# Gate and up products of six FFNs with weight tiles stationary, tokens moving in turns from two halves

## The reference, cut to what matters

```python
def _rmsnorm(x, g):
    x32 = x.astype(jnp.float32)
    y = x32 * lax.rsqrt(jnp.mean(x32 * x32, axis=-1, keepdims=True) + NORM_EPS)
    return (y * g.astype(jnp.float32)).astype(x.dtype)

def _swiglu(h, w_gate_up, w_down):
    gu = jnp.einsum('bsd,df->bsf', h, w_gate_up)
    g, u = gu[..., :FF], gu[..., FF:]
    return jnp.einsum('bsf,fd->bsd', jax.nn.silu(g) * u, w_down)
```

## Time and profile before

| | us |
|---|---|
| median of 3 runs | 1983.0 (1982.34 to 1984.53) |
| the profiled execution, its own time | 1981.93 |
| its span in the profile | 1979.7 |
| PE busy, share of the span | 1947.5 (98%) |
| PE weight loads busy | 1684.7 (85%) |
| DVE, ACT busy | 1233.1 (62%), 1109.0 (56%) |

### The profile page before, as it was taken

The page is one execution under the profiler, slowest core; times in us unless marked ns, Lnnn a source line. Parts: engine busy times, 40 slices in busy tenths (PEclk is TensorE's granted clock), DMA queues, the critical chain, the costliest instruction groups (busy, mean ns, idle before and its releaser), DMA issues.

```text
span 1979.7 us, 25169 instructions
## 1 busy us (share of the span) xinstructions
PE 1947.5 (98%) x9627; PEld 1684.7 (85%) x9627; DVE 1233.1 (62%) x1721; ACT 1109.0 (56%) x1682; POOL 36.3 (2%) x60
## 2 busy tenths in 40 slices
PE   8999999999999999999999999999999999999999
PEld 7888888888888888888887888888888888888888
DVE  6576665565767655655567765655555566756653
ACT  6576555455765644645467665554454466665552
POOL 0000100000000000000000000000000000000000
PEclk9999999999999999999999999999999999999999
DMA  7555666555556665566664345665666664545663
GB/s 261 163 158 171 188 198 194 196 183 174 155 177 204 200 199 197 186 202 192 197 174 144 123 160 158 188 196 196 197 192 197 197 192 138 181 143 167 195 198 138
DMA packets 258214, 359.76 MB, mean 182 GB/s; under 512 B 16908, under 2 KB 152288, under 8 KB 258096
## 3 DMA queue, kind: packets, MB, share of 16 engines
q1 hardware_dynamic: 256016, 352.75, 56.1%
q0 software_dynamic: 2080, 5.41, 0.9%
HBM read 357.04 MB, written 1.06 MB: 181 GB/s over the span
## 4 chain that ended last, share of the span: by engine, by line
PE 90%; DVE 5%; ACT 3%; issue 1%; POOL 1%; DMA 0%; SPq 0%; DVEq 0%; ACTq 0%
PE M L801 27%; PE M L803 27%; PE M L802 27%; PE AUX L843 3%; DVE WL L1303 2%; ACT WH L1082 1%; PE AUX L857 1%; PE AUX L1055 1%; PE AUX L1033 1%; PE AUX L979 1%; DVE SM L1452 1%; ACT TMP L1115 0%; DVE TMP L1409 0%; PE AUX L994 0%; PE AUX L985 0%
## 5 line engine op out<-in xcount | busy, mean ns | idle before, releaser
L1303 DVE TENSOR_TENSOR WL<-RAW,WH 128x1024 fp32r<-128x1024 f32 x669 | 815.7, 1222 | 583.1 <-ACT WH L1082 580.1
L1082 ACT ACTIVATE WH<-RAW 128x1024 fp32r<-128x1024 f32 x669 | 704.8, 1055 | 591.5 <-PE M L803 583.0
L801 PE MATMUL M<-WH,Bh 128*128 128x512 f32 x1792 | 698.7, 390 | 2.3 <-DVE WL L1303 2.3
L802 PE MATMUL M<-WL,Bh 128*128 128x512 f32 x1792 | 680.0, 379 | 0.0
L803 PE MATMUL M<-WH,Bl 128*128 128x512 f32 x1792 | 679.9, 379 | 0.0
L801 PEld LDWEIGHTS M<-WH,Bh 128*128 128x128 f32 x1792 | 339.4, 189 | 49.2 <-DVE WL L1303 2.8
L803 PEld LDWEIGHTS M<-WH,Bl 128*128 128x128 f32 x1792 | 339.2, 189 | 48.2
L802 PEld LDWEIGHTS M<-WL,Bh 128*128 128x128 f32 x1792 | 339.8, 190 | 42.6
L1111 ACT ACTIVATE AS<-M,KEEP 128x256 f32<-128x256 f32 x132 | 55.4, 471 | 93.1 <-PE M L803 89.4
L801 PE MATMUL M<-WH,MTh 128*128 128x512 f32 x128 | 53.0, 414 | 0.0
L802 PE MATMUL M<-WL,MTh 128*128 128x512 f32 x128 | 48.5, 379 | 0.0
(11 more groups left out here) (415 smaller groups left out, 2496.5 us busy)
## 6 DMA issues: line engine op xcount, KB each, us to landing
RAW<-in_ffn_w_in SPq DMA_DIRECT2D x352, 256.0 KB, 3.3
RAW<-in_w_in SPq DMA_DIRECT2D x104, 512.0 KB, 3.6
RAW<-in_w_gate_up SPq DMA_DIRECT2D x176, 256.0 KB, 3.3
RAW<-in_ffn_w_out SPq DMA_DIRECT2D x88, 512.0 KB, 3.8
RAW<-in_w_down SPq DMA_DIRECT2D x44, 512.0 KB, 3.8
RAW<-in_x_w_kv SPq DMA_DIRECT2D x32, 512.0 KB, 3.6
RAW<-in_even_w_in SPq DMA_DIRECT2D x24, 512.0 KB, 3.8
RAW<-in_odd_w_in SPq DMA_DIRECT2D x24, 512.0 KB, 4.0
```

What stands on the lines that cost most here:

```text
L801: e.matmul(out, s.hi, wh, start=s.at0, stop=False)
L802: e.matmul(out, s.hi, wl, start=False, stop=False)
L1082: e.activation(p.WH[:, h, 0:s.size], p.RAW[:, i, 0:s.size], ACT.Copy).then_inc(k.w_hi, 1)
L1303: e.tensor_tensor(p.WL[:, h, 0:s.size], p.RAW[:, s.u % NRAW, 0:s.size], hi.bitcast(F32), ALU.subtract).then_inc(k.w_lo, 1)
```

## The change

The gate and up products of all six FFNs change roles. The stationary operand is a 128x128 tile of weights, the moving one is all 256 tokens of B for one kt. One kt is then 4 weight tiles (`s.t` is gate or up, `j` one of two tiles of 128 columns) by 3 matmuls of 256 columns, 12 in all. The result has hidden columns on partitions, as the down product needs it, and the transposes of the hidden values are gone. The tokens move by turns from the two halves of 128 (`woven`), except in the FFN named f2a0 (the second FFN of layer 0 of the second block), where they move in plain sequence.

As tokens now lie on the free axis, r can't be a scalar of a partition. A step `rb` makes a tile RB with r of all tokens on every partition: two float32 matmuls with r as a broadcast stationary operand against the identity, in PE's list at 3.5 kt after the norm, and a copy on ACT. DVE multiplies the gate part with RB, ACT takes Silu in place, DVE multiplies by the up part (without r), ACT writes the high part and DVE the low part. The r of the up part is applied in the residual step, per token, together with the scale. The memory tokens and the last norm's gain are loaded into TMP buffers instead of tiles of their own.

```diff
+    def chunk_w(self, name, region, nk, lab):
+
+
+        self.bank_use[2 * self.pair] += 1
+        self.bank_use[2 * self.pair + 1] += 1
+        c = Chunk(name, self.pair, [self.bank_use[2 * self.pair], self.bank_use[2 * self.pair + 1]])
+        self.pair ^= 1
+        kt = 0
+        while kt < nk:
+            u = self.unit(name)
+            kn, ncol, _ = self.units[u]
+            for kk in range(kn):
+                for half in range(2):
+                    s = self.add("mw", self.now + 0.5 * half, 3)
+                    s.c, s.kt, s.u, s.kk, s.t, s.ncol = c, kt, u, kk, half, ncol
+                    s.at0, s.final = kt == 0, kt == nk - 1
+                    s.unit_end = half == 1 and kk == kn - 1
+                    s.src = self.made[lab, kt]
+                    s.hi, s.lo = (x[:, kt, :] for x in region)
+                    c.mms.append(s)
+                kt += 1
+                self.now += 1
+            c.done = u + 1
+        c.end = self.now
+        return c
+
...
             s = self.add("ff", c.end, 0)
-            s.c, s.norm, s.i = c, self.norms[lab_in], c_
-            s.silu = [self.AS[:, (c_ % 2) * 2 + t, 0:256] for t in range(T)]
-            s.h = [HB[:, (c_ % 3) * 2 + t, :] for t in range(T)]
-            blocks = [s.h[t][:, q * P:(q + 1) * P] for q in range(2) for t in range(T)]
-            self.turn(c.end + 2.0, "bank", s, blocks, A, 2 * c_, None, lab_mid, 2 * c_)
-        self.residual(down, A, KF, lab_mid, scale, gain, lab_next, final=final)
+            f = self.add("fh", c.end + 1.2)
+            o = self.add("fl", c.end + 2.6)
+            s.c, s.rb, s.past, s.g = c, rb, past[c_ % 2], HB[:, c_ % 2, :]
+            f.c, f.s, f.past, f.h = c, s, past[c_ % 2], HB[:, 2 + c_ % 2, :]
+            o.f = f
+            f.hi, o.lo = (x[:, 2 * c_:2 * c_ + 2, :].rearrange("p k c -> p (k c)") for x in A)
+            past[c_ % 2] = o
+            for q in range(2):
+                self.made[lab_mid, 2 * c_ + q] = o
+        self.residual(down, A, KF, lab_mid, rb, gain, lab_next, final=final)
...
+        elif s.kind == "mw":
+            c = s.c
+            h = s.u % NHL
+            if s.kk == 0 and s.t == 0:
+                e.wait_ge(k.w_lo, s.u + 1)
+            if s.src not in seen:
+                seen.add(s.src)
+                e.wait_ge(k.aux_out[s.src.bank], s.src.use)
+            if s.at0 and c.use[s.t] > 1:
+                e.wait_ge(k.m_out[c.banks[s.t]], c.use[s.t] - 1)
+            for j in range(2):
+                out = p.M[c.banks[s.t]][:, 256 * j:256 * j + 256]
+                row = slice(s.kk * s.ncol, (s.kk + 1) * s.ncol)
+                name = p.unit_names[s.u]
+                wh, wl = (x[:, h, row][:, 256 * s.t + P * j:256 * s.t + P * j + P] for x in (p.WH, p.WL))
+                xh, xl = (x if name == "f2a0" else woven(x) for x in (s.hi, s.lo))
+                e.matmul(out, wh, xh, start=s.at0 and j == 0, stop=False)
+                e.matmul(out, wh, xl, start=False, stop=False)
+                i = e.matmul(out, wl, xh, start=False, stop=s.final and j == 1)
+            if s.unit_end:
+                i.then_inc(k.w_used, 1)
+        elif s.kind == "rb":
+            e.wait_ge(k.r_made, s.norm.n)
+            if s.use > 1:
+                e.wait_ge(k.aux_out[b], s.use - 1)
+            for t in range(T):
+                i = e.matmul(aux[:, t * P:(t + 1) * P], s.norm.r[:, t:t + 1].to_broadcast([P, P]), ident, start=True, stop=True)
+            i.then_inc(k.aux_full[b], 1)
...
-                e.activation(s.silu[t], banks[t][:, 0, :], ACT.Silu, scale=r[t]).then_inc(k.silu_made, 1)
+            e.wait_ge(k.m_out[s.c.banks[0]], s.c.use[0])
+            e.activation(s.g, s.g, ACT.Silu).then_inc(k.silu_made, 1)
+        elif s.kind == "fh":
+            e.wait_ge(k.m_out[s.c.banks[1]], s.c.use[1])
+            e.activation(s.hi, s.h, ACT.Copy).then_inc(k.ff_hi, 1)
+        elif s.kind == "rb":
+            e.wait_ge(k.aux_full[b], s.use)
+            e.activation(p.RB, aux[:, 0:T * P], ACT.Copy).then_inc(k.aux_out[b], 1)
...
         elif s.kind == "res":
+            if s.rb is not None:
+                e.wait_ge(k.rs_made, s.rb.n)
             for t in range(T):
                 x = halves(p.X[:, t, s.half * 512:(s.half + 1) * 512])
-                e.scalar_tensor_tensor(out=x, in0=banks[t], scalar=s.scale, in1=x, op0=ALU.mult,
+                f = 1.0 if s.rb is None else s.rb.rs[:, t:t + 1]
+                e.scalar_tensor_tensor(out=x, in0=banks[t], scalar=f, in1=x, op0=ALU.mult,
...
         elif s.kind == "ff":
-            for t in range(T):
-                e.wait_ge(k.silu_made, 2 * (s.n - 1) + t + 1)
-                e.scalar_tensor_tensor(out=s.h[t], in0=banks[t][:, 1, :], scalar=r[t], in1=s.silu[t], op0=ALU.mult,
-                                       op1=ALU.mult).then_inc(k.m_out[c.banks[t]], 1)
+            if s.past is not None:
+                q = s.past.f.c
+                e.wait_ge(k.m_out[q.banks[1]], q.use[1])
+            e.wait_ge(k.aux_out[s.rb.bank], s.rb.use)
+            rb = p.RB.rearrange("p (h i) -> p h i", h=2).unsqueeze(1).to_broadcast([P, 2, 2, P])
+            tiles, apart_tiles = (tiles_n, apart_n) if s.n in p.natural else (tiles_w, apart_w)
+            rb = rb if s.n not in p.natural else p.RB.unsqueeze(1).to_broadcast([P, 2, 256])
+            e.tensor_tensor(tiles(s.g), apart_tiles(p.M[c.banks[0]]), rb, ALU.mult).then_inc(k.m_out[c.banks[0]], 1)
+        elif s.kind == "fh":
+            if s.past is not None:
+                e.wait_ge(k.ff_lo, s.past.n)
+            e.wait_ge(k.silu_made, s.s.n)
+            tiles, apart_tiles = (tiles_n, apart_n) if s.n in p.natural else (tiles_w, apart_w)
+            e.tensor_tensor(tiles(s.h), apart_tiles(p.M[c.banks[1]]), tiles(s.s.g), ALU.mult).then_inc(k.m_out[c.banks[1]], 1)
+        elif s.kind == "fl":
+            e.wait_ge(k.ff_hi, s.f.n)
+            e.tensor_tensor(s.lo, s.f.h, s.f.hi.bitcast(F32), ALU.subtract).then_inc(k.ff_lo, 1)
+        elif s.kind == "rb":
+            e.tensor_scalar(s.rs, s.norm.r, s.scale, None, ALU.mult).then_inc(k.rs_made, 1)
...
-                    e.dma_start(s.MX[:, t, n * 512:(n + 1) * 512],
+                    e.dma_start(p.TMP[2 * t + n],
...
-                e.dma_start(p.NF[:, n * 512:(n + 1) * 512],
+                e.dma_start(p.TMP[4 + n],
```

More of the change, by code:

```diff
@@ L176, in halves, with apart_w, apart_n, tiles_n @@
     return x.rearrange("p (h i) -> p h i", h=2)
+def apart_w(bank):
+    return bank[:, :].rearrange("p (j i h) -> p j h i", j=2, h=2)
+def apart_n(bank):
+    return bank[:, :].rearrange("p (j c) -> p j c", j=2)
+def tiles_n(x):
+    return x.rearrange("p (j c) -> p j c", j=2)
+def tiles_w(x):
+    return x.rearrange("p (j h i) -> p j h i", j=2, h=2)
 BANKED = ("turn", "tq", "ret_s", "ret_o", "st_z", "st_s", "st_o", "cu1", "cu2", "df_s", "pt", "df_o", "hg_s", "hg_o",
-          "cx_s", "cx_pt", "cx_o", "gains")
+          "cx_s", "cx_pt", "cx_o", "gains", "rb")
 HALVED = ("turn", "st_o", "hg_o", "cx_o")
 LATER = {
-    "conv": (0.0, 0.9), "turn": (0.5, 1.0), "tq": (0.5, 0.0), "gains": (0.5, 1.0), "rope": (0.0, 0.6), "ff": (0.0, 0.5),
+    "conv": (0.0, 0.9), "turn": (0.5, 1.0), "tq": (0.5, 0.0), "gains": (0.5, 1.0), "rope": (0.0, 0.6), "ff": (0.7, 0.0), "fh": (0.7, 0.0), "rb": (0.4, 0.0),
     "hq": (0.0, 1.3), "ret_s": (0.0, 0.7), "ret_o": (0.9, 1.5), "rg": (0.0, 0.6), "st_z": (0.7, 1.9), "st_p": (0.0, 0.5),
@@ L349, in turn_x, with residual @@
             self.norm(at + (2.5 if gain is not None else 0.5), lab, sq, ss)
-    def residual(self, name, region, nk, lab, scale, gain, lab_next, final=False):
+    def residual(self, name, region, nk, lab, rb, gain, lab_next, final=False):
         ss = self.small(4)
@@ L362, in residual @@
             s = self.add("res", c.end, 0)
-            s.c, s.half, s.scale = c, n, scale
+            s.c, s.half, s.rb = c, n, rb
             if final:
@@ L369, in ffn @@
     def ffn(self, gate, down, lab_in, lab_mid, scale, gain, lab_next, A, HB, final=False):
+        nm = self.norms[lab_in]
+        rb = self.add("rb", nm.at + 3.5)
+        rb.norm, rb.scale, rb.rs = nm, scale, self.small(T)
+        past = [None, None]
         for c_ in range(FF // 256):
-            c = self.chunk(gate, self.B, 0, KD, lab_in)
+            c = self.chunk_w(gate, self.B, KD, lab_in)
             s = self.add("ff", c.end, 0)
-            s.c, s.norm, s.i = c, self.norms[lab_in], c_
-            s.silu = [self.AS[:, (c_ % 2) * 2 + t, 0:256] for t in range(T)]
-            s.h = [HB[:, (c_ % 3) * 2 + t, :] for t in range(T)]
-            blocks = [s.h[t][:, q * P:(q + 1) * P] for q in range(2) for t in range(T)]
-            self.turn(c.end + 2.0, "bank", s, blocks, A, 2 * c_, None, lab_mid, 2 * c_)
-        self.residual(down, A, KF, lab_mid, scale, gain, lab_next, final=final)
+            f = self.add("fh", c.end + 1.2)
[8 more added lines that the diff above has]
```

(41 more changed lines are left out.)

1 line of the change is left out of this document (removed).

## The result

The changed kernel takes 1991.0 us (median of 6, 1989.8 to 1991.8) against 1982.7 for the kernel before in the same comparison (6 runs). The ratio is 1.0039, 95% interval 1.0026 to 1.0052: slower by 0.4%, or 8 us. The profiled execution has a span of 1989.5 against 1979.7.

What follows compares the result with a forecast made beforehand. PE was taken to bound the kernel through the time from one matmul to the next. The terms -28.8 - 2.1 + 2.7 + 3.6 + 21.1 + 9.2 gave +5.7 us, a median of 1988.7, range 1972 to 2014.

Steps and rivals of the forecast that it cites:

- the likeliest case: The whole kernel at the summed forecast, with or without a half clock: 1988.7 us, own range 1983 to 1995, chance 0.60.
- Turns: Gate and up parts: 66 turns of four transposes each, 0.436 a turn, are removed from PE: -28.8 us.
- Waits at turns: First turns of two FFNs: PE no longer waits for DVE's values, 1.41 and 0.70: -2.1 us.
- rb's matmuls: Each FFN's rb step: two float32 matmuls, run as two each, add 0.45 per FFN: +2.7 us.
- The wait at rb: First FFN: PE stands at rb until POOL, issuing small DMAs first, has written r: +3.6 us.
- Rival 4: First FFN: PE's clock falls in rb's wait, adding 2 to 3 us: 1991; no separate chance, inside the 0.60 case.
- Woven pace: Five woven FFNs: 256-column matmuls take 0.112 each, two replacing one of 0.216: +21.1 us.
- The second rival: Gate and up matmuls: load stays hidden, PE bound by the stream at 0.109: 1974, 0.5% faster; chance 0.20.
- Plain pace: f2a0, in plain sequence: 256-column matmuls take 0.1167 each, as the narrow matmuls do: +9.2 us.
- since these move the same tile: f2a0: ground for giving its matmuls the narrow matmuls' 0.1167, as both move B in plain sequence.
- The first rival: All six FFNs: weaving doesn't help at 128 columns, so all run at 0.1167: +24.6 more, 2013; chance 0.14.
- DVE and ACT at nothing: Gate and up chunks: DVE's 27 us of extra work is covered by 583 us idle before its splits, costing nothing.

Runs made afterwards that it cites:

- e7: e3 plus four transposes of the identity per gate and up chunk where the turns were, results unused; 2008.7 us, ratio 1.0132 to the kernel before.
- e3: Changed kernel with f2a0 woven too and POOL making r of the first FFN before its small loads; 1977.2 us, ratio 0.9970 to the kernel before.
- e2: Changed kernel with POOL making r of the first FFN before issuing its small loads; 1987.2 us, ratio 1.0018 to the kernel before.
- e1: Changed kernel with f2a0's tokens woven like the other FFNs; 1983.5 us, ratio 1.0001 to the kernel before.
- e4: Changed kernel with gate and up matmuls moving 240 columns instead of 256, loads and counts the same; 1983.7 us in one run.
- e5: Changed kernel with all six FFNs moving tokens in plain sequence; 2033.6 us, ratio 1.0256 to the kernel before.
- e6: Changed kernel with five FFNs moving even tokens, then odd ones, f2a0 still plain; 2594.4 us in one run.
- e8: e3 with tokens by turns from places 64, 32, 16, 8, 4 or 2 columns apart, one distance per FFN; 1985.8 us in one run.

## Why the prediction was right, point by point

The forecast was +5.7 us on the kernel before, and the runs show +8.3, inside the likeliest case's own range (1983 to 1995) and on the side forecast. The mechanism was right: the weight load takes back most of what the transposes gave. That the number came so near is in part luck, since two costs were put too low (3.5 and 1.7) and two others erred the other way (1.6 and 0.7).

- **Turns, -28.8:** held. e7 puts them back for 28.8 in the FFNs.
- **Waits at turns, -2.1:** held, as far as it can be read alone. gu0 without its new wait (e3) gained 1.48, where 1.41 was counted. f1a0 gained 1.39, of which 0.70 was counted; the other 0.7 is the wait at line 857, which the sum did not have.
- **rb's matmuls, +2.7:** held. In e2 the four matmuls at 243.84 are 0.11 apart.
- **The wait at rb, +3.6:** held, 3.49, with POOL as releaser. It came from counting places in PE's and POOL's lists, not from any row that showed a wait.
- **Rival 4, the half clock, 2 to 3 us:** happened, and cost 1.7. It was given inside the likeliest case but not put into the sum. The two levels that the prediction names in GHz stand in the traces as granted clocks of 1.00 and 0.50. At 1.00 matmuls of 512 columns start 0.216 apart, 2.4 columns a ns, and at 0.50 0.427 apart, 1.2 columns a ns (e1, from 1692.19 to 1693.90: 1.71 for four).
- **Woven pace, 0.112:** held, 0.1117, so +19.5 in place of +21.1. The 0.112 is the distance that loads keep in the float32 rows, 0.111 to 0.112, and e4 and the distances between loads in the changed kernel's trace bear out that it paces these matmuls too. The second rival is out. Its 0.109 (0.2184 for two) was an estimate, and in no run did an FFN go at that pace. Woven matmuls with a load of 0.19 took 0.1117 (e3: 111 or 112 ns), the transposes with their loads of 0.14 took 0.109, and half of the 0.216 of 512 columns is 0.108. The 2.7 ns from 0.109 to 0.1117 are worth 5280 x 0.0027 = 14 us here, more than the whole result.
- **Plain pace, 0.1167:** the term that was mis-sized. f2a0 ran at 0.120, so it cost 528 x (0.240 - 0.216) = 12.7 in place of 9.2. The step that failed is "since these move the same tile": the narrow matmuls move it with a load of 8 columns beside them, these with one of 128. e4 shows that the plain pace follows the number of moving columns (16 fewer took off 0.0080), so it is the reading that slowed, by 3% against the narrow matmuls. Whether the large load beside it is why was not tested.
- **The first rival** (weaving over 128 columns doesn't help) is out by e1 and e5.
- **DVE and ACT at nothing:** held, the new matmuls waited 0.0 for WL. DVE's extra work was 36 and not 27 us, and the idle time before its splits covered it.

With the measured terms the sum is -28.8 - 2.1 + 2.7 + 3.5 + 1.7 + 19.5 + 12.7 = +9.2, and +8.5 with the wait at line 857. The FFNs of the trace show +8.8 and the medians +8.3.

## What to carry to other kernels

Making weights stationary and moving only 256 columns gave up the cover over the weight load: here a matmul of 256 columns costs 0.1117 where half of one of 512 costs 0.108, and that ate 19.5 of the 28.8 us of the transposes in five FFNs (it would be 23.4 in six). A new step in an in-order list waits for the latest of its inputs, so look up when each input is made before placing it (r came 3.5 us late because POOL issued small loads first); moving those loads and weaving the sixth FFN turned a loss of 0.4% into a gain of 0.3%. The order in which fp32r columns are read is a price of its own, here 0.1117 to 0.233 a matmul, and it must be measured for the order used.

## What the runs showed of the hardware that was not expected

- The order of the moving fp32r columns sets the pace by up to a factor of two: 0.1117 by turns from two places at least 4 columns apart, 0.120 in plain sequence, 0.227 with a step of 2, 0.22 to 0.23 with steps of 4 to 32, 0.14 with a step of 64. In e6 this cost 600 us.
- Two places by turns are fast if they are at least 4 columns apart; four places (0.14) and eight (0.22) are not.
- The wait of 3.5 us brought the granted clock from 1.0 to 0.50, and it stood there until 2.5 us after the product had started again. The half clock also followed rb's wait in the profiles of e1, e4 and e5.
- Shorter waits did so in some executions and not in others. The wait of 2.28, which left the pace as it was in the kernel before, was followed by a clock of 0.50 in 4 of the 11 profiles (e1, e2, e4 and e7), at 1.6 to 1.7 us each. Another of 2.0, for a DVE result between f1a0 and f2a0, was followed by it in 5 of the 11 (e2, e5, e6, e7 and e8). So the length of these waits alone doesn't tell whether the clock falls, and executions of one kernel differ in it: the mean granted clock of the kernel before was 1.000 in some runs and 0.998 in others.
- Pairs of a 128-column weight load and a woven 256-column matmul start 111.7 ns apart, and just the same with 240 columns.
